# A two-layer hybrid attention trunk: attention in pairs of steps, masks added by VectorE, the last token block of the norm tails in halves

## What is computed

```python
for i in range(DEPTH):                          # 2 layers
    h = rms_norm(x, g_mix_pre[i])
    z = h @ w_in[i]
    ya = blocked_attention(aq, ak, av, A_HEAD_DIM ** -0.5, True, log_f_cum)    # FoX, per-frame causal
    yb = blocked_attention(qb, kb, vb, (B_NOPE + B_ROPE) ** -0.5, False)       # MLA, chunk causal
    yc = banded_sink_attention(cq, ck, cv, sink[i], rel_bias)                  # sliding window
    gates = jax.nn.sigmoid(h @ w_gate[i] + b_gate[i])
    merged = ga * (ya @ w_branch_a[i]) + gb * (yb @ w_branch_b[i]) + gc * (yc @ w_branch_c[i])
    x = x + rms_norm(merged @ w_out[i], g_mix_post[i])                         # tail n = 0
    u = causal_dwconv(rms_norm(x, g_ffn_pre[i]) @ w_up[i], conv_w[i], conv_b[i])
    x = x + rms_norm((gelu(ug) * uv) @ w_down[i], g_ffn_post[i])               # tail n = 1
    pg = jax.nn.sigmoid(rms_norm(x, g_ple_pre[i]) @ w_ple_gate[i])
    x = x + rms_norm(pg * (p[i] @ w_ple[i]), g_ple_post[i])                    # tail n = 2
```

## Time and profile before

| | us |
|---|---|
| time before, median of 3 runs | 2012.74 (2012.43 to 2012.76) |
| the profiled execution's own time | 2011.93 |
| its span in the trace | 2010.1 |
| PE busy in the span | 1954.9 |
| DVE busy | 1106.0 |
| ACT busy | 815.2 |
| POOL busy | 107.6 |

### The profile page before, as it was taken

How to read it: one execution, slowest core, us unless ns; L and a number is a source line. 1 busy time by engine, 2 the same in 40 slices (tenths; PEclk the granted TensorE clock), 3 DMA queues, 4 the chain that set the end, 5 groups by cost and what they waited for, 6 DMA issues and landing times.

```text
span 2010.1 us, 26179 instructions
## 1 busy us (share of the span) xinstructions
PE 1954.9 (97%) x9397; PEld 1599.2 (80%) x9397; DVE 1106.0 (55%) x1955; ACT 815.2 (41%) x1403; POOL 107.6 (5%) x83
## 2 busy tenths in 40 slices
PE   8999999999999999999989999999999999999997
PEld 6877877778878888888867778777788788888886
DVE  5444446534567677425674445455445777763266
ACT  4244435443344444314433444354433444442243
POOL 0000000101101111000000000001010011110000
PEclk9999999999999999999999999999999999999999
DMA  5411233212613333332343112321135133333322
GB/s 153 111 35 50 63 85 84 60 46 84 199 32 100 99 94 94 99 122 94 80 127 89 32 53 61 87 84 53 52 126 158 35 102 94 98 100 115 95 85 73
DMA packets 256437, 176.06 MB, mean 88 GB/s; under 512 B 52149, under 2 KB 240465, under 8 KB 256081
## 3 DMA queue, kind: packets, MB, share of 16 engines
q1 hardware_dynamic: 256200, 174.56, 29.7%
q10 hardware_dynamic: 136, 0.16, 0.1%
HBM read 170.31 MB, written 4.36 MB: 87 GB/s over the span
## 4 chain that ended last, share of the span: by engine, by line
PE 88%; DVE 6%; issue 3%; ACT 3%; DMA 0%; SPq 0%; DVEq 0%; ACTq 0%
PE psum L598 76%; PE psum L782 4%; PE psum L756 3%; PE psum L770 2%; ACT wh L1012 1%; PE psum L760 1%; DVE xt L1394 1%; PE psum L644 1%; DVE mx L1424 1%; PE psum L791 1%; DVE yg_down L1386 0%; DVE oP L1375 0%; ACT Pr L1065 0%; ACT PT L1077 0%; DVE xnl L1319 0%
## 5 line engine op out<-in xcount | busy, mean ns | idle before, releaser
L598 PE MATMUL psum<-xnh,wh 128*128 128x512 f32 (+1 forms) x1424 | 574.0, 403 | 9.1 <-DVE kC L1535 2.3
L598 PE MATMUL psum<-xnh,wl 128*128 128x512 f32 (+1 forms) x1424 | 557.4, 391 | 0.0
L598 PE MATMUL psum<-xnl,wh 128*128 128x512 f32 (+1 forms) x1424 | 556.5, 391 | 0.0
L1305 DVE TENSOR_TENSOR wl<-raw,wh 128x1024 fp32r<-128x1024 f32 (+1 forms) x276 | 364.4, 1320 | 318.6 <-ACT wh L1012 318.0
L1012 ACT ACTIVATE wh<-raw 128x1024 fp32r<-128x1024 f32 (+1 forms) x276 | 291.2, 1055 | 452.8 <-PE psum L598 444.7
L598 PEld LDWEIGHTS psum<-xnh,wh 128*128 128x128 f32 (+1 forms) x1424 | 267.8, 188 | 68.6 <-issue 16.2
L598 PEld LDWEIGHTS psum<-xnh,wl 128*128 128x128 f32 (+1 forms) x1424 | 267.0, 188 | 58.8 <-issue 0.2
L598 PEld LDWEIGHTS psum<-xnl,wh 128*128 128x128 f32 (+1 forms) x1424 | 268.0, 188 | 50.1 <-issue 0.2
L1424 DVE TENSOR_REDUCE mx<-psum 128x1 f32<-128x128 f32 (+3 forms) x128 | 62.6, 489 | 148.5 <-PE psum L757 135.1
L598 PE MATMUL psum<-wh,fh 128*128 128x512 f32 x288 | 112.0, 389 | 0.0
L598 PE MATMUL psum<-wh,fl 128*128 128x512 f32 x288 | 112.0, 389 | 0.0
(11 more groups left out here) (248 smaller groups left out, 2945.1 us busy)
## 6 DMA issues: line engine op xcount, KB each, us to landing
raw<-in_w_up_dram SPq DMA_DIRECT2D x88, 512.0 KB, 3.7
raw<-in_w_gate_dram SPq DMA_DIRECT2D x48, 512.0 KB, 3.6
raw<-in_w_down_dram SPq DMA_DIRECT2D x44, 512.0 KB, 3.5
raw<-in_w_in_dram SPq DMA_DIRECT2D x40, 512.0 KB, 3.6
raw<-in_w_out_dram SPq DMA_DIRECT2D x16, 512.0 KB, 3.6
raw<-in_w_ple_gate_dram SPq DMA_DIRECT2D x16, 512.0 KB, 3.6
raw<-in_w_in_dram SPq DMA_DIRECT2D x16, 256.0 KB, 3.4
raw<-in_w_branch_a_dram SPq DMA_DIRECT2D x8, 512.0 KB, 3.3
```

The lines of the kernel that those rows point to most:

```text
L598: ins = pe.matmul(out, left, right, start=start and n == 0, stop=stop and n == 2)
L1305: dve.tensor_tensor(low[:, 0:n], raw[(L * NCH + c) % RAW][:, 0:n], hi[:, 0:n].bitcast(F32), ALU.subtract).then_inc(w_lo.sem, 1)
```

## The change

- **Turns in pairs.** The table has GROUPS = 21 turns g instead of 38, on the same places: g * 48 // 21 and g * 96 // 21. At turn g PE does S(2g), S(2g+1), T(2g-3), T(2g-2), V(2g-5), V(2g-4), and Y at g = 7, 11, 15, 19. ACT does the exponentials of 2g-1 and 2g and then the copies PT of 2g-3 and 2g-2. DVE does the maxima of 2g and 2g+1, then at g = 6, 10, 14, 18 `ytok`, and at g = 8, 12, 16, 20 `yl`.
- **Masks.** The mask matmuls are gone. DVE's instruction that adds and reduces (L1419, now L1469) is used in all three attentions: it adds mask or bias, takes the minimum of the negated sum and writes the negated scores to `Sp`. The exponential always reads `Sp`. S(s) now waits for `max_done` of step s - 2 instead of `exp_done`. L1425 is left in MLA alone.
- **Mask memory.** The masks lie as f32 [128, 2, 512] in the memory of `ptok`; a DMA brings the 128 columns in every layer, and POOL zeroes the other 384 of each behind its own `qA` memset.
- **Tails.** Only the last token block is done in two halves of 512 columns: squares, gain product, addition to x and handing over. PE's `turn` of this block waits for the first half before k = 0 and for the second before k = 4. The inverse root has 9 small instructions instead of 12. The last output DMA is in two parts.

```diff
-ATT_STEPS = STEPS + 6
+GROUPS = STEPS // 2 + 5
...
+def parts(t):
+    return [slice(0, D)] if t < TB - 1 else [slice(0, D // 2), slice(D // 2, D)]
...
+def pair(n):
+    return [s for s in (n, n + 1) if 0 <= s < STEPS]
...
@@ PE, attention
-            if s < STEPS:
+            for s in pair(2 * g):
...
-                    pe.wait_ge(exp_done.sem, exp_done.at(L, n + s - 1))
+                    pe.wait_ge(max_done.sem, max_done.at(L, n + s - 1))
...
-                if a != 1:
-                    pe.matmul(o[:, 0:nk(i)], q, k, start=True, stop=False)
-                    pe.matmul(o[:, P * i:P * i + P], identb, maskA if a == 0 else maskB,
-                              start=False, stop=True).then_inc(s_full.sem, 1)
-                else:
-                    pe.matmul(o[:, 0:nk(i)], q, k, start=True, stop=True).then_inc(s_full.sem, 1)
-            if 2 <= s <= STEPS + 1:
-                u = s - 2
+                pe.matmul(o[:, 0:nk(i)], q, k, start=True, stop=True).then_inc(s_full.sem, 1)
+            for u in pair(2 * g - 3):
...
-            if 3 <= s <= STEPS + 2:
-                u = s - 3
+            for u in pair(2 * g - 5):
...
-            if s >= 5 and (s - 5) % H == H - 1:
-                i = (s - 5) // H
+            if g >= 7 and g % 4 == 3:
+                i = (g - 7) // 4
@@ ACT, attention
-                src = Sp[s % 2] if a == 1 else SB[s % 2]
-                scale = rq[:, i:i + 1] if a == 2 else 1.0
+                scale = nrq[:, i:i + 1] if a == 2 else -1.0
...
-                act.activation(Pr[s % 2][:, c0:c0 + nk], src[:, 0:nk], ACT.Exp, bias=nm[:, i % 2, h:h + 1],
+                act.activation(Pr[s % 2][:, c0:c0 + nk], Sp[s % 2][:, 0:nk], ACT.Exp, bias=nm[:, i % 2, h:h + 1],
@@ DVE, inverse_root_of_block, the last block's first step
+                link(L, dve.scalar_tensor_tensor(out=w, in0=ysum[:, one], scalar=0.5 * EPS, in1=ysum[:, TB:TB + 1],
+                                                 op0=ALU.add, op1=ALU.add))
@@ DVE, residual
+            for h, cols in enumerate(parts(t)):
...
+                dve.scalar_tensor_tensor(out=xt[:, t, cols], in0=g[:, cols], scalar=rpost[:, t:t + 1],
+                                         in1=xt[:, t, cols], op0=ALU.mult, op1=ALU.add).then_inc(x_ready.sem, 1)
@@ DVE, attention
-                    link(L, dve.tensor_reduce(m, b[:, 0:nk], AX_X, ALU.max))
...
+                added = biasC[:, h, c0:c0 + nk] if a == 1 else masks[:, a // 2, T - nk:T]
+                low = dve.tensor_tensor_reduce(out=Sp[s % 2][:, 0:nk], in0=b[:, 0:nk], in1=added, scale=-1.0,
+                                               scalar=nsink[:, h:h + 1] if a == 1 else -NEG, op0=ALU.add, op1=ALU.min,
+                                               accum_out=m if a == 2 else neg)
...
@@ POOL
             pool.memset(qA[HD:HD + 1, :, :], 1.0).then_inc(ones_set.sem, 1)
+            pool.wait_ge(ones_set.sem, ones_set.at(L, 1))
+            pool.memset(masks[:, :, 0:T - P], 0.0).then_inc(mask_zero.sem, 1)
```

More of the change, by code:

```diff
@@ L28 @@
 F32R = mybir.dt.float32r
-BF16 = mybir.dt.bfloat16
 I32 = mybir.dt.int32
@@ L1050, in x_sum, with attention @@
             act.activation(junk[1][:, :], xt[:, t, :], ACT.Square, accum_out=xsum[:, t:t + 1]).then_inc(x_summed.sem, 1)
-        def attention(L, a, s):
+        def attention(L, a, g):
             n = STEPS * a
-            if s < STEPS:
+            for s in pair(2 * g - 1):
                 i, h = s // H, s % H
@@ L1273, in _ @@
                 block_wait(L, 2, t)
-                act.activation(thP[t % 2][:, :], wide_of[t], ACT.Tanh, scale=rhalf[:, t:t + 1]).then_inc(pg_gated.sem, 1)
-                act.wait_ge(o_ready.sem, o_ready.at(L, t + 1))
+                for cols in parts(t):
+                    act.activation(thP[t % 2][:, cols], wide_of[t][:, cols], ACT.Tanh, scale=rhalf[:, t:t + 1]
+                                   ).then_inc(pg_gated.sem, 1)
                 y_sum(L, 2, t, oP[t % 2][:, :], sq_down)
@@ L1386, in residual @@
-            dve.tensor_tensor(g[:, :], src, GAIN[n][:, :], ALU.mult).then_inc(gained.sem, 1)
-            if n == 2:
-                dve.wait_ge(y_summed.sem, y_summed.at(L, TB * n + t + 1))
-            link(L, dve.tensor_scalar(rtmp[:, 0, one], ysum[:, one], 1.0 / D, EPS, ALU.mult, ALU.add))
-            link(L, inverse_root(L, one, rpost[:, one]))
-            dve.wait_ge(gained.sem, gained.at(L, TB * n + t + 1))
+                for h, cols in enumerate(parts(t)):
+                    dve.wait_ge(pg_gated.sem, pg_gated.at(L, done(0, t, h)))
+                    dve.scalar_tensor_tensor(out=oP[t % 2][:, cols], in0=thP[t % 2][:, cols], scalar=1.0,
+                                             in1=pl[:, t, cols], op0=ALU.add, op1=ALU.mult).then_inc(o_ready.sem, 1)
@@ new lines, in residual @@
+                dve.wait_ge(o_ready.sem, o_ready.at(L, done(0, t, 0)))
+                with_gain(oP[t % 2], parts(t)[0])
+            elif t < TB - 1:
+                dve.wait_ge(block_full.sem, block_full.at(L, (TB - 1) * n + t + 1))
+                dve.wait_ge(y_summed.sem, y_summed.at(L, whole))
+                with_gain(wide_of[t], parts(t)[0])
+            else:
+                dve.wait_ge(w_used.sem, w_used.at(L, (ST_UP, ST_PLE)[n]))
+                with_gain(wide_of[t], parts(t)[1])
+                dve.wait_ge(y_summed.sem, y_summed.at(L, done(n, t, 0)))
+                with_gain(wide_of[t], parts(t)[0])
@@ L1392, in residual @@
+            dve.wait_ge(y_summed.sem, y_summed.at(L, whole))
+            inverse_root_of_block(L, t)
             if n == 0 and t == 0:
                 dve.wait_ge(x_back.sem, x_back.at(L, 16))
-            dve.scalar_tensor_tensor(out=xt[:, t, :], in0=g[:, :], scalar=rpost[:, one], in1=xt[:, t, :],
-                                     op0=ALU.mult, op1=ALU.add).then_inc(x_ready.sem, 1)
-        def attention(L, a, s):
+            for h, cols in enumerate(parts(t)):
+                if n == 2 and h:
+                    dve.wait_ge(o_ready.sem, o_ready.at(L, done(0, t)))
+                    with_gain(oP[t % 2], cols)
+                dve.wait_ge(gained.sem, gained.at(L, done(n, t, h) if n == 2 else whole))
+                dve.scalar_tensor_tensor(out=xt[:, t, cols], in0=g[:, cols], scalar=rpost[:, t:t + 1],
+                                         in1=xt[:, t, cols], op0=ALU.mult, op1=ALU.add).then_inc(x_ready.sem, 1)
```

160 lines of the change are left out of this document (86 added, 74 removed).

## The result

The changed kernel takes **2054.02 us** (median of 4 runs, 2053.13 to 2056.35), the kernel before 2012.59 (2010.90 to 2012.76, 4 runs). The ratio is 1.021, with a 95% interval of 1.0192 to 1.0227: 41.4 us slower. The direction was forecast, the size was not: 2021 us, with a range of 1988 to 2033. The profiled execution took 2056.35 us, its span is 2054.6, 44.5 more than the span before.

What follows compares the result with a forecast made beforehand. PE was taken to bound the kernel (88% of the span). Stops +28.2, masks -7.6, switches -3.8, tails, mask memory and clock summed to +8.4 us on 2011.93: 2020.3, as a median 2021 us; range 1988 to 2033.

Steps and rivals of the forecast that it cites:

- Old stops: PE's waits in the three attentions before the change, largest kind T waiting for `y_lo`: all go, -21.4 us in both layers.
- New stop 1: Attention turns 8 and 12: T(14) waits behind T(13), exp(15), max(17) and yl in a chain; +28.6 us.
- Rival A: exp(15) and max(17) do not wait for T(13), so T(14) waits 0.05 to 0.3; 1990 us, chance 0.12.
- New stop 2: Turns 7, 11 and 15: Y waits for a bank that ACT copies only behind two exponentials; +10.6 us.
- New stop 3: Turn 16 of sliding window and MLA: T(30) waits for yl behind `post` and `wl` of a new chunk; +5.3 us.
- Tail n = 0: Last block's shorter root, half of the gain product earlier, PE starting on half of x: -1.8 us a layer, -3.6.
- Tail n = 2 and the end: Shorter block work on DVE and half of x at the end, plus a smaller last DMA: together -4.8 us.
- The granted clock: Half-clock dips at the tails vanish, -4.6 us; two of twelve long attention stops are followed by one, +3 us.
- Rival C: The clock falls behind each of twelve long attention stops, 12 x 1.7 instead of 3: +17, 2038 us, chance 0.08.
- B: Rival: all attention stops vanish, since products have a whole turn to arrive and Y's bank is free; 1968 us, chance 0.05.
- E: Rival: New stop 1 at half its price, exp and max partly overlapping PE's own attention work; 2007 us, chance 0.11.
- D: Rival: the matmuls taken away give nothing, what waits behind them being an engine's latency; 2032 us, chance 0.12.

Runs made afterwards that it cites:

- u1_steps: The changed kernel with the pairing undone: one step a turn at the old distances, masks by VectorE, exponentials from Sp and new tails kept; 1992.98 us.
- u6_late_inter: The changed kernel with yl made at the end of the Y turn and ScalarE alternating exponential and copy; 1985.08 us.
- u5_yl_late: The changed kernel with yl made at the end of the turn that does Y (7, 11, 15, 19) instead of the next; 1993.38 us.
- u7_steps_whole: u1_steps with the last token block of the tails whole again instead of in halves, the nine-step root kept; 1998.98 us.
- u2_yl_first: The changed kernel with VectorE making yl ahead of the two masked maxima in turns 8, 12, 16 and 20; 2004.21 us.
- u4_interleave: The changed kernel with ScalarE alternating exponential and copy in each turn instead of two exponentials, then two copies; 2041.81 us.
- u8_lone_fox12: u6_late_inter with yl of FoX's query block 1 made behind the maxima of turn 12 again, one stop per layer; 1998.92 us.

## Why the prediction was wrong in size

Point by point, in its own order, between the two profiled executions.

- **Masks, -7.6: right in kind**, -8.6 by u1_steps. **Switches, -3.8: right**, 0.036 to 0.039 each (u6_late_inter, u5_yl_late) against 0.037. Together they are 1.0 more than forecast.
- **Old stops, 21.4, gone: right**, but for the waits that were forecast to be kept.
- **New stop 1, 28.6: right within 0.11 us** in every place: 2.30, 2.54, 2.11, 2.11, 2.63, 2.87 a layer, 29.1 in both, against 2.3, 2.5, 2.0, 2.0, 2.6, 2.9. (Its links were off in both directions: the masked maximum over 384 columns takes 0.56 instead of 0.62, and starts 0.21 behind the exponential's row sum instead of 0.05.) Rival A falls with the timeline: exp(15) starts 0.38 behind T(13).
- **New stop 2, 10.6: right**, 5.7 a layer with the first place at a chunk's start the longest (0.98, 1.15, 1.33). **New stop 3, 5.3: too small**, 1.59 and 2.25, 7.7 in both. The bank waits of the branch chunks that I held to be kept (5.1 for both layers with the first score matmul) grew from 1.4 to 3.7 a layer, 8.0 with it. A wait of 0.6 a layer for `ytok` was not foreseen. All new stops: 28.7 a layer, 57.5 against the 49.6 forecast. Over the whole stretches PE's stops grew from 15.1 to 33.4 a layer, 36.7 in both, where the forecast had 28.2: 8.5 more.
- **Tail n = 0, -3.6: about right**, -2.0 and -1.5 up to the turn behind tail n = 1, a little of it clock. **Tail n = 1, +0.8: not there**; from its first turn to the gate's PE takes what it took. **Tail n = 2 and the end, -4.8: too large.** The transposes behind tail n = 2 end 1.2 earlier, but 12 dense matmuls at half clock follow where there were 2, and FoX of layer 1 starts with nothing gained; the program's end comes 1.3 closer. The halves gave nothing there (u7_steps_whole): what PE's first wait got shorter came back as a second wait.
- **Mask memory, +0.8:** POOL's second memset took 0.74 us and the instruction of VectorE beside it 0.76. Its share in the time was not isolated. The masked maxima did not wait for POOL: the two that ran beside its merging in the changed kernel took 0.56 us, as the thirty others over 384 columns did.
- **The granted clock, -4.6 at the tails and +3 in the attentions: the step that failed.** Behind tail n = 0 the stop was shorter, 1.65 instead of 2.63 (0.9 was forecast), but the clock fell nevertheless: 7 dense matmuls at half clock where there were 9. The transposes behind the stop and the first dense matmuls, 0.43 apart:

```profile
599.25 1.32 PE L664 MATMUL psum<-cst,xt 128*128 128x128 f32 x8 [1.65 <-DVE xt L1440]
601.23 0.77 PE L618 MATMUL psum<-xnh,wh 128*128 128x512 f32 x1 [0.67 <-DVE xnl L1340]
601.79 0.63 PE L618 MATMUL psum<-xnl,wh 128*128 128x512 f32 x1
602.22 0.63 PE L618 MATMUL psum<-xnh,wl 128*128 128x512 f32 x1
```

Part of that was the luck of the execution. The changed kernel and the nine experiments with halves have this same stop in 20 places, and the clock fell in 9 of them (in both layers here, in neither in u2_yl_first, u4_interleave, u5_yl_late and u6_late_inter). No row of the trace showed such a stop with the clock left alone at that place; the term rested on an argument alone. In the attentions I let two of twelve stops pay, 1.5 us each. Seven of the twelve paid in the trace (none of the four in turn 16), and in FoX the clock was at 0.50 for 17 us in each layer, which cost about 8. The bill is 24 us (u5_yl_late).

The sum closes on the profiled executions: 2020.3 us forecast, 8.5 more of stops, 21 more of clock in the attentions, 4 of the tails' clock that wasn't given back, 0.6 at tail n = 0 and 2.3 at the other tails, the memset and the two ends of the program, less 1.0 for masks and switches, make 2055.7, beside 2056.35 measured. (That execution is 2.3 above the median of 2054.02.)

**Rival C** (2038) named the cause and still gave too little: it took 1.7 us for each of twelve stops, a price that no row shows (the tail's own was 2.3). Seven paid, 24 us, 3.4 each on average. In FoX the slow stretch ran over 15 dense matmuls and the widest turns of attention. The stops of the kernel before that were as long as the new ones or longer, 2.63 us and 4.42 us, both had half clock behind them, the first in the earlier trace rows and the second here:

```profile
1010.00:1013.00 3.00, 2.69 (x10) 1.96 (x11) 1.71 (x4) 2.35 (x5) 0.00 (x0) 0.50 0.67 262
```

These rows should have carried the likeliest case; I gave it 0.08, because PE had been less busy ahead of them, and the range ended at 2033.

**The other rivals.** B (no stops) and E (stop 1 at half its price) fall with the stops as measured. D (the matmuls taken away give nothing) falls with u1_steps, 11.0 us shorter in the attentions for 2.4 us of shorter stops.

The Trainium skill ("TensorE: Matmul & The Clock Gate", A second HAM failure mode: psum-queue depth-cycling) describes such a loss for a kernel that takes PSUM banks in turn and pauses shortly between groups. The traces here agree in kind: each of the slow stretches in the attentions stands behind a wait for a bank of two. They disagree with "each stop pays", which I made of it: stops of 2.1 us mostly don't.

**What is open.** Why the clock stays at half for 6.8 us in one layer and 17.1 in the other behind the same stop (u8_lone_fox12), and why the same stops are followed by it 7 times in one kernel and 12 times in another (u4_interleave), was not settled. No run here varied the length of one stop in small steps at one place, and one execution of each kernel was traced.

## What to carry to other kernels

When two steps are put in one turn, write down for every buffer of two who frees it and in which order the engine that frees it stands: pairing brought a transpose, an exponential, a maximum and a copy out into one chain of 2.4 us only because `yl` stood two instructions too late, and moving one block gave back 61 us, more than the 41 that the change had cost. Price a stop of TensorE of about 2 us or more at its length plus a stretch at half clock (36 of 52 such stops had one here), and take the upper end of that stretch into the range. A busy share of 100% says nothing of the clock; look at the clock column and at instructions per microsecond.

## What the runs showed of the hardware

In the twelve traces (before, after and the ten experiments) PE has 86 stops of 1.3 us or more at attention work. What its clock did within 8 us behind them went by the length of the stop (the distance between two matmuls less the usual one):

| stop, us | places | followed by granted clock 0.50 |
|---|---|---|
| 1.3 to 1.8 | 34 | 1 |
| 2.1 | 16 | 5 |
| 2.25 to 2.30 | 14 | 10 |
| 2.54 | 6 | 6 |
| 2.63 to 2.87 | 16 | 15 |

At half clock a dense matmul starts every 0.43 us instead of 0.227. Ahead of these stops and behind them PE had dense work and was busy but for shorter stops; of the 2.63 at tail n = 0 that can't be said.

The table doesn't prove that length alone decides. Each length belongs to one kind of place: 2.1 is turn 8 or 12 of the sliding window, 2.54 turn 12 of FoX, 2.63 to 2.87 turns 8 and 12 of MLA, 2.25 to 2.30 turn 16 of MLA and turn 8 of FoX. And at tail n = 0, where PE does transposes just ahead of the stop and not dense work, a stop of 1.8 us by the same measure (1.65 idle) was followed by 0.50 in 9 of 20 places, where the attentions have 1 of 34 for 1.3 to 1.8.
